# Products of split float32: one 512-column matmul into both halves of a bank in place of two of 256

## Chip, cores and metric

The kernel runs on one core of a Trainium2 chip. The metric is the device time of one execution in microseconds. The core's engines are TensorE (PE, with its weight loads shown as PEld), VectorE (DVE), ScalarE (ACT), GpSimd (POOL) and SyncE (SP, which here only issues DMAs). They run side by side and are ordered by semaphores.

## The reference

A stack of two blocks on 256 tokens of width 1024, all in float32. The first block does twice (depth 2): a half-weighted SwiGLU layer, a mixer (a gated recurrence in depth 0, a spatial gating in depth 1), and a second SwiGLU layer. The second block puts 16 meta tokens ahead (272 rows) and does two layers of windowed attention beside an mLSTM. Most of the arithmetic is in dense products with weights:

```python
def swiglu(x, w_in, w_out):                 # w_in 1024 x 5632, w_out 2816 x 1024
    g, u = jnp.split(x @ w_in, 2, axis=-1)
    return (jax.nn.silu(g) * u) @ w_out

h = h + 0.5 * swiglu(rms_norm(h, ffn1_norm[i]), ffn1_w_in[i], ffn1_w_out[i])
h = h + mixer(rms_norm(h, mix_norm[i]))
h = h + 0.5 * swiglu(rms_norm(h, ffn2_norm[i]), ffn2_w_in[i], ffn2_w_out[i])
```

## The kernel before

**Layout.** Everything is transposed: features on the 128 partitions, tokens on the free axis. The residual `h` holds 8 chunks of 128 features. The norm's gain is applied to the activations and its reciprocal root (`rstd`, one value a token) after the product.

**Split products.** A float32 value is held as two fp32r parts, hi and lo. A product takes three matmuls a block of 128 rows (k): w_hi with x_hi, w_hi with x_lo, w_lo with x_hi, all added in one PSUM tile of 256 (or 272) columns (L526 to L528). Each brings its own weight load. Activations lie in `x_hi`, `x_lo` (input of a layer) and `y_hi`, `y_lo` (input of an output product).

**Units and pairs.** `plan()` cuts all weights into 456 units of up to 4 k blocks x 256 columns, and a pair of output tiles (T = 2 pair + m, m = 0, 1) takes the units of its 256 columns one after another: two units in a gate/up pair, six (4, 4, 4, 4, 3, 3 blocks) in an FFN output pair. Tile T lies in bank T mod 4, so a bank comes back after two pairs; PE then waits for `tile_read`. `first_done` tells that tile m = 0 of a pair is complete, `unit_done` that a unit is.

**Weights.** SP loads a unit into a ring of 4 (`raw`) once the lo part of the unit that had the slot is made. ACT makes w_hi by a cast (L925), three units ahead of PE and not before PE is done with the slot; DVE makes w_lo = raw - w_hi (L1439); PE waits for `lo_made`.

**Gate/up turns.** A phase `in..` is 11 turns of a gate pair and an up pair (the first turn written out, the others a hardware loop on each engine). In a turn DVE multiplies the two gate tiles with rstd (L1479), ACT takes the silu (L961), POOL multiplies it with rstd (L1325), DVE multiplies the up tiles with that (L1495), ACT rounds the result to y_hi (L971) and DVE makes y_lo (L1502). Between them each of ACT and DVE handles four units of weights in a written-out order.

**Output phases.** `out..`, `rec_out`, `sg_out` and `proj..`: for each tile DVE adds the scaled tile to `h` (L1524, an STT), ACT makes x_hi of the next layer (L932) and DVE x_lo (L1452). After the last chunk the sum of squares goes through PE (L552, L554), a root on ACT (L950) and a reciprocal on DVE (L1457).

**Phases in order:** in01, out01, rec_b, rec_a, rec_out, in02, out02, in11, out11, sg_b, sg_a, sg_out, in12, out12, then for each of two layers kv, mif, aq, mqk, mv, mo, ag, mg (with attention and mLSTM steps between the units) and proj0 or proj1. Products from kv to proj0 have 272 columns in part; those of proj1 have 256.

## Time and profile before

| | |
|---|---|
| times of three runs | 1570.74, 1567.24, 1570.32 us |
| median | 1570.32 us |
| profiled execution, first to last instruction | 1566.5 us |
| around that span, by the median | 3.8 us |
| PE / DVE / ACT / POOL busy | 97 / 67 / 49 / 18% of the span |
| read from HBM | 237.21 MB, 152 GB/s over the span |

The profile lists one profiled execution by its span; its own total, with what lies around the span, is not listed apart, and the table gives the difference to the median instead. Matmuls are pipelined: the duration of one (280 ns) overlaps the next ones, so PE's pace is read from the times at which matmuls start, or from how many fall into a stretch. The granted clock of TensorE has two levels here, 1.00 (2.4 GHz) and 0.50 (1.2 GHz). An idle time is put down to what ended it.

### The profile page before, as it was taken

To read this page: it belongs to the slowest core of one execution; us is meant where nothing else is said; L and a number is where in the kernel's file an instruction comes from. 1 tells how busy PE (TensorE), PEld (TensorE's weight loads), DVE (VectorE), ACT (ScalarE), POOL (GpSimd) and SP (SyncE) were. 2 spreads that over 40 slices of the span, in tenths; PEclk is the share of its full clock that TensorE was granted. 3 is DMA by queue.
4 is the path that set the end of the run, shared out by engine and by line. 5 is a ranking of instruction groups with operands and counts; after the bars stand their busy time and mean duration, and the time that the engine had idled before them with its cause. 6 is when DMAs were issued, how large, how long until landed. Compare 5 with 4: busy or idle time off the path is not lost.

```text
span 1566.5 us, 31432 instructions
## 1 busy us (share of the span) xinstructions
PE 1522.4 (97%) x11949; PEld 1463.1 (93%) x11949; DVE 1051.3 (67%) x1997; ACT 768.2 (49%) x1274; POOL 289.2 (18%) x350
## 2 busy tenths in 40 slices
PE   7999998999999999999999998999999999999998
PEld 6999998999999999999999997888898999888898
DVE  6666579766656665567766556896678678765783
ACT  5544457554535454454545434446544453564442
POOL 4111112211111111131311023432100124321000
PEclk9999999999999999999999998999999999999999
DMA  6556753465555655554665553433333543333333
GB/s 202 188 180 197 242 164 122 150 199 179 177 188 173 190 180 182 181 177 134 189 187 182 175 180 94 139 106 95 96 95 108 176 143 115 95 95 109 98 120 120
DMA packets 245275, 239.65 MB, mean 153 GB/s; under 512 B 15160, under 2 KB 244392, under 8 KB 245048
## 3 DMA queue, kind: packets, MB, share of 16 engines
q1 hardware_dynamic: 245176, 238.29, 48.5%
q8 instruction: 67, 1.10, 0.3%
q14 instruction: 32, 0.26, 0.1%
HBM read 237.21 MB, written 1.05 MB: 152 GB/s over the span
## 4 chain that ended last, share of the span: by engine, by line
PE 85%; DVE 10%; ACT 2%; issue 2%; POOL 1%; DMA 0%; SPq 0%; DVEq 0%; ACTq 0%; POOLq 0%
PE bank L526 25%; PE bank L528 25%; PE bank L527 25%; DVE w_lo L1439 2%; PE bank L842 1%; PE bank L801 1%; PE bank L780 1%; PE bank L779 1%; ACT w_hi L925 1%; PE bank L760 1%; DVE work L1592 1%; DVE work L1479 1%; PE bank L847 1%; PE bank L856 0%; PE bank L812 0%
## 5 line engine op out<-in xcount | busy, mean ns | idle before, releaser
L1439 DVE TENSOR_TENSOR w_lo<-raw,w_hi 128x1024 fp32r<-128x1024 f32 (+1 forms) x456 | 556.6, 1229 | 319.0 <-ACT w_hi L925 318.8
L526 PE MATMUL bank<-x_hi,w_hi 128*128 128x256 f32 (+1 forms) x2480 | 722.7, 291 | 6.7 <-DVE x_lo L1452 5.2
L528 PE MATMUL bank<-x_hi,w_lo 128*128 128x256 f32 (+1 forms) x2480 | 709.5, 286 | 0.0
L527 PE MATMUL bank<-x_lo,w_hi 128*128 128x256 f32 (+1 forms) x2480 | 708.7, 286 | 0.0
L925 ACT CAST w_hi<-raw 128x1024 fp32r<-128x1024 f32 (+1 forms) x456 | 465.3, 1029 | 275.9 <-PE bank L528 261.2
L526 PEld LDWEIGHTS bank<-x_hi,w_hi 128*128 128x128 f32 x2480 | 478.2, 193 | 15.8 <-issue 10.9
L527 PEld LDWEIGHTS bank<-x_lo,w_hi 128*128 128x128 f32 x2480 | 478.7, 193 | 0.8
L528 PEld LDWEIGHTS bank<-x_hi,w_lo 128*128 128x128 f32 x2480 | 478.1, 193 | 0.0
L526 PE MATMUL bank<-y_hi,w_hi 128*128 128x256 f32 (+1 forms) x1088 | 311.0, 286 | 8.1 <-DVE y_lo L1450 8.1
L528 PE MATMUL bank<-y_hi,w_lo 128*128 128x256 f32 (+1 forms) x1088 | 310.1, 285 | 0.0
L527 PE MATMUL bank<-y_lo,w_hi 128*128 128x256 f32 (+1 forms) x1088 | 310.0, 285 | 0.0
L526 PEld LDWEIGHTS bank<-y_hi,w_hi 128*128 128x128 f32 x1088 | 209.7, 193 | 9.1 <-DVE w_lo L1439 4.4
L528 PEld LDWEIGHTS bank<-y_hi,w_lo 128*128 128x128 f32 x1088 | 209.8, 193 | 0.0
L527 PEld LDWEIGHTS bank<-y_lo,w_hi 128*128 128x128 f32 x1088 | 209.8, 193 | 0.0
L1325 POOL TENSOR_TENSOR work<-work,rstd 128x256 f32<-128x256 f32 x88 | 63.5, 741 | 417.5 <-ACT work L961 417.5
L1479 DVE TENSOR_TENSOR work<-bank,rstd 128x256 f32<-128x256 f32 (+1 forms) x204 | 82.3, 423 | 21.7 <-PE bank L528 21.2
L971 ACT CAST y_hi<-work 128x256 f32 (+1 forms) x88 | 35.5, 407 | 89.0 <-DVE work L1495 89.0
L961 ACT ACTIVATE work<-work 128x256 f32<-128x256 f32 x88 | 36.0, 418 | 78.5 <-DVE work L1479 78.5
L1306 POOL TENSOR_TENSOR sq<-h 128x256 f32<-128x256 f32 (+1 forms) x48 | 33.4, 696 | 200.2 <-DVE h L1524 197.7
L932 ACT ACTIVATE x_hi<-h,par 128x256 fp32r<-128x256 f32 (+1 forms) x64 | 32.7, 512 | 69.9 <-DVE h L1524 62.3
L1452 DVE SCALAR_TENSOR_TENSOR x_lo<-h,par,x_hi 128x256 fp32r<-128x256 f32 (+1 forms) x64 | 36.3, 569 | 29.5 <-ACT x_hi L932 29.4
L1304 POOL TENSOR_TENSOR sumsq<-h 128x256 f32<-128x256 f32 (+1 forms) x8 | 4.9, 616 | 253.9 <-DVE h L1524 245.9
(259 smaller groups left out, 1244.5 us busy)
## 6 DMA issues: line engine op xcount, KB each, us to landing
raw<-in_ffn_w_in_dram SPq DMA_DIRECT2D x176, 512.0 KB, 3.6
raw<-in_w_in_dram SPq DMA_DIRECT2D x100, 512.0 KB, 3.4
raw<-in_ffn_w_out_dram SPq DMA_DIRECT2D x64, 512.0 KB, 3.8
raw<-in_w_out_dram SPq DMA_DIRECT2D x32, 512.0 KB, 3.5
raw<-in_ffn_w_out_dram SPq DMA_DIRECT2D x32, 384.0 KB, 3.0
raw<-in_rec_w_in_dram SPq DMA_DIRECT2D x16, 512.0 KB, 3.3
raw<-in_sg_w_in_dram SPq DMA_DIRECT2D x16, 512.0 KB, 3.3
raw<-in_rec_w_out_dram SPq DMA_DIRECT2D x8, 512.0 KB, 3.4
```

The lines of the kernel that those rows point to most:

```text
L526: mm(acc, wh, xh, start=first and j == 0, stop=False)
L527: mm(acc, wh, xl, start=False, stop=False)
L528: i_ = mm(acc, wl, xh, start=False, stop=last and j == n - 1)
L925: nc.scalar.copy(w_hi[:, s, 0:n, :], raw[:, s, 0:n, :]).then_inc(hi_made, 1)
L932: i_ = activation(xview(dst, k, N), src, ACT.Copy, scale=scale)
L961: activation(ffn_s[:, m, :], ffn_t[:, m, :], ACT.Silu).then_inc(silu_done, 1)
L971: nc.scalar.copy(dst, ffn_h[:, m, :]).then_inc(act_hi, 1)
L1306: link(TT(sq[:, T0:L], src(c), src(c), MUL))
L1325: TT(ffn_r[:, m, :], ffn_s[:, m, :], rstd[:, META:L], MUL).then_inc(gate_scaled, 1)
L1439: TT(w_lo[:, s, 0:n, :], raw[:, s, 0:n, :], w_hi[:, s, 0:n, :].bitcast(fp32), SUB).then_inc(lo_made, 1)
L1452: i_ = STT(out=xview(dst_lo, k, N), in0=src, scalar=scale, in1=hi, op0=MUL, op1=SUB)
L1479: TT(dst, tile(pr, m, N), rstd[:, T0:L], MUL).then_inc(tile_read, 1)
```

## The change

Eleven phases are marked (`HALVES`): the four gate/up phases, the four FFN output phases, rec_out, sg_out and proj1. In a marked pair a k block takes two matmuls: w_hi with hi and lo of the activations side by side, 512 columns over a whole bank, and w_lo with hi, 256 columns, into the upper half of the bank. The result of a tile is the sum of both halves of its bank. For this x_hi and x_lo become two rows of one tensor `x_s`, and y_hi and y_lo of `y_s`.

In a gate/up turn ACT copies the upper half ("low" terms) to SBUF and DVE adds it to the lower half, for gate and up tiles. Both products with rstd and with the gate then run on POOL: POOL has six products a turn where it had two. In an output phase DVE adds the two halves to `h` in two linked STTs.

```diff
+HALVES = set()
+for _n in ("in01", "out01", "rec_out", "in02", "out02", "in11", "out11", "sg_out", "in12", "out12", f"proj{DEPTH - 1}"):
+    _, _b, _k = PHASES[_n]
+    HALVES.update(range(_b, _b + _k))
...
-        x_hi = sb("x_hi", [P, NC8 * L], fp32r)
-        x_lo = sb("x_lo", [P, NC8 * L], fp32r)
-        y_hi = sb("y_hi", [P, NF * SEQ], fp32r)
-        y_lo = sb("y_lo", [P, NF * SEQ], fp32r)
+        x_s = sb("x_s", [P, 2, NC8 * L], fp32r)
+        y_s = sb("y_s", [P, 2, NF * SEQ], fp32r)
+        x_hi, x_lo = x_s[:, 0, :], x_s[:, 1, :]
+        y_hi, y_lo = y_s[:, 0, :], y_s[:, 1, :]
...
-                        if N == SEQ and wide_x:
-                            xh, xl = (t[:, k * L + META:(k + 1) * L] for t in (hi, lo))
+                        cols = slice(k * L + META, (k + 1) * L) if N == SEQ and wide_x else slice(k * N, (k + 1) * N)
+                        opens, closes = first and j == 0, last and j == n - 1
+                        if pair in HALVES:
+                            both = bank[T % 4][:, :].rearrange("p (h n) -> p h n", h=2)
+                            small = bank[T % 4][:, SEQ:2 * SEQ]
+                            if opens:
+                                mm(both, wh, xs[:, :, cols], start=True, stop=False)
+                                mm(small, wl, xs[:, 0, cols], start=False, stop=False)
+                            else:
+                                mm(small, wl, xs[:, 0, cols], start=False, stop=False)
+                                i_ = mm(both, wh, xs[:, :, cols], start=False, stop=closes)
                         else:
-                            xh, xl = xview(hi, k, N), xview(lo, k, N)
-                        mm(acc, wh, xh, start=first and j == 0, stop=False)
-                        mm(acc, wh, xl, start=False, stop=False)
-                        i_ = mm(acc, wl, xh, start=False, stop=last and j == n - 1)
+                            acc = bank[T % 4][:, 0:N]
+                            mm(acc, wh, xs[:, 0, cols], start=opens, stop=False)
+                            mm(acc, wh, xs[:, 1, cols], start=False, stop=False)
+                            i_ = mm(acc, wl, xs[:, 0, cols], start=False, stop=closes)
...
-            def gate_turn(pb, ub, i, first=None):
-
-                o4, o = 4 * i, (4 * i if not isinstance(i, int) else 4 * i)
+            def low_half(pr, m, i, f, dst):
+
+                U = units_of(pr)[-1][0] + 1
+                if m == 0:
+                    act.wait_ge(first_done, FIRSTS[pr] + 1 + 2 * i)
+                else:
+                    act.wait_ge(unit_done, U + 4 * i)
+                nc.scalar.copy(dst, bank[(2 * pr + m) % 4][:, SEQ:2 * SEQ]).then_inc(low_out, 1)
+
+            def gate_turn(ub, i, f, first=None):
+                pb, count = PHASES[IN_OF[f]][1], SPLITS["y_out" + IN_OF[f][2:]]
+
+                o = 4 * i
                 for U in (ub, ub + 1):
                     split_w(U + LEAD, o)
                 if first is not None:
                     root(first, META)
                 for m in range(2):
-                    act.wait_ge(tile_read, 2 * pb + m + 1 + o4)
+                    low_half(pb, m, i, f, ffn_s[:, m, :])
+                for m in range(2):
+                    act.wait_ge(gate_normed, 22 * f + m + 1 + 2 * i)
                     activation(ffn_s[:, m, :], ffn_t[:, m, :], ACT.Silu).then_inc(silu_done, 1)
                 for U in (ub + 2, ub + 3):
                     split_w(U + LEAD, o)
                 for m in range(2):
-                    act.wait_ge(tile_read, 2 * pb + 2 + m + 1 + o4)
+                    act.wait_ge(act_ready, count + m - 1 + 2 * i)
+                    low_half(pb + 1, m, i, f, ffn_h[:, m, :])
+                for m in range(2):
+                    act.wait_ge(gated_up, 22 * f + m + 1 + 2 * i)
...
                 def turn(i):
+                    for m in range(2):
+                        pool.wait_ge(tile_read, 2 * pb + m + 1 + 4 * i)
+                        TT(ffn_t[:, m, :], ffn_t[:, m, :], rstd[:, META:L], MUL).then_inc(gate_normed, 1)
                     for m in range(2):
                         pool.wait_ge(silu_done, 22 * f + m + 1 + 2 * i)
                         TT(ffn_r[:, m, :], ffn_s[:, m, :], rstd[:, META:L], MUL).then_inc(gate_scaled, 1)
+                    for m in range(2):
+                        pool.wait_ge(tile_read, 2 * pb + 2 + m + 1 + 4 * i)
+                        pool.wait_ge(gate_scaled, 22 * f + m + 1 + 2 * i)
+                        pool.wait_ge(act_ready, count + m - 1 + 2 * i)
+                        TT(ffn_h[:, m, :], ffn_t[:, m, :], ffn_r[:, m, :], MUL).then_inc(gated_up, 1)
...
-                    scaled(pb, m, ffn_t[:, m, :], SEQ, META, o)
+                    dve.wait_ge(low_out, 44 * f + m + 1 + 4 * i)
+                    if f or not isinstance(i, int):
+                        dve.wait_ge(gated_up, 22 * f + m - 1 + 2 * i)
+                    TT(ffn_t[:, m, :], tile(pb, m, SEQ), ffn_s[:, m, :], ADD).then_inc(tile_read, 1)
                 for U in (ub + 2, ub + 3):
                     split_w(U + LEAD, o)
                 for m in range(2):
-                    wait_tile(pb + 1, m, o)
-                    dve.wait_ge(gate_scaled, 22 * f + m + 1 + 2 * i)
-                    TT(ffn_h[:, m, :], tile(pb + 1, m, SEQ), ffn_r[:, m, :], MUL).then_inc(tile_read, 1)
+                    dve.wait_ge(low_out, 44 * f + m + 3 + 4 * i)
+                    dve.wait_ge(silu_done, 22 * f + m + 1 + 2 * i)
+                    TT(ffn_t[:, m, :], tile(pb + 1, m, SEQ), ffn_h[:, m, :], ADD).then_inc(tile_read, 1)
...
-                        STT(out=h[:, c, T0:L], in0=tile(pb + p, m, N), scalar=half, in1=h[:, c, T0:L], op0=MUL,
-                            op1=ADD).then_inc(tile_read, 1)
+                        i_ = STT(out=h[:, c, T0:L], in0=tile(pb + p, m, N), scalar=half, in1=h[:, c, T0:L], op0=MUL, op1=ADD)
+                        if pb + p in HALVES:
+                            link(i_)
+                            i_ = STT(out=h[:, c, T0:L], in0=low(pb + p, m), scalar=half, in1=h[:, c, T0:L], op0=MUL, op1=ADD)
+                        i_.then_inc(tile_read, 1)
```

**PE, the first tile of the program's first marked pair.** Before, three matmuls of 256 columns a k block (two blocks shown):

```order
L526 MATMUL bank<-x_hi,w_hi 128x256
L527 MATMUL bank<-x_lo,w_hi 128x256
L528 MATMUL bank<-x_hi,w_lo 128x256
L526 MATMUL bank<-x_hi,w_hi 128x256
L527 MATMUL bank<-x_lo,w_hi 128x256
L528 MATMUL bank<-x_hi,w_lo 128x256
```

and now, in the same place (the first three blocks):

```order
L532 MATMUL bank<-x_s,w_hi 128x512
L533 MATMUL bank<-x_s,w_lo 128x256
L535 MATMUL bank<-x_s,w_lo 128x256
L536 MATMUL bank<-x_s,w_hi 128x512
L535 MATMUL bank<-x_s,w_lo 128x256
L536 MATMUL bank<-x_s,w_hi 128x512
```

The first block opens the bank with the 512-column matmul; from the second on the 256-column one (w_lo) comes first and the 512-column one (w_hi) closes. One matmul and one weight load a block are gone.

**ACT, the first gate/up turn.** `work` holds all small tiles of the FFN. Before, from the root of the norm on:

```order
L950 ACTIVATE rms<-bank,epsc 128x256
L961 ACT_TABLE_LOAD
L961 ACTIVATE work<-work 128x256 x2
L925 CAST w_hi<-raw 128x1024 x2
L971 CAST y_hi<-work 128x256 x2
```

and now:

```order
L972 ACTIVATE rms<-bank,epsc 128x256
L981 COPY work<-bank 128x256 x2
L995 ACT_TABLE_LOAD
L995 ACTIVATE work<-work 128x256 x2
L947 CAST w_hi<-raw 128x1024 x2
L981 COPY work<-bank 128x256 x2
L1008 CAST y_s<-work 128x256 x2
```

Two copies out of a bank stand ahead of the silu of the gate tiles, and two ahead of the cast to y_hi. The two casts of weights (w_hi) still come between, behind the silu.

**POOL, the loop over turns.** Before:

```order
L1326 ISA
L1325 TENSOR_TENSOR work<-work,rstd 128x256
L1324 REGISTER_ALU
L1325 TENSOR_TENSOR work<-work,rstd 128x256
L1326 REGISTER_ALU
L1326 COMPARE_AND_BRANCH
```

and now, up to the first of the last two products:

```order
L1373 ISA
L1364 TENSOR_TENSOR work<-work,rstd 128x256
L1363 REGISTER_ALU
L1364 TENSOR_TENSOR work<-work,rstd 128x256
L1366 ISA
L1367 TENSOR_TENSOR work<-work,rstd 128x256
L1366 REGISTER_ALU
L1367 TENSOR_TENSOR work<-work,rstd 128x256
L1369 REGISTER_ALU
L1371 REGISTER_ALU
L1372 TENSOR_TENSOR work<-work 128x256
L1369 REGISTER_ALU
```

The product of the gate tiles with rstd (L1364) has moved here from DVE and now stands ahead of ACT's silu; the product of silu with rstd (L1367) was here before; the product with the up tiles (L1372) has moved here too and stands ahead of ACT's cast to y_hi.

## Rows read from the trace of the kernel before

**Rows 1.** The page, part 1: busy us, share of span, instructions of each engine.

```profile
PE 1522.4 (97%) x11949; PEld 1463.1 (93%) x11949; DVE 1051.3 (67%) x1997; ACT 768.2 (49%) x1274; POOL 289.2 (18%) x350
```

**Rows 2.** The page, part 4: the chain that ended last, share by engine.

```profile
PE 85%; DVE 10%; ACT 2%; issue 2%; POOL 1%; DMA 0%; SPq 0%; DVEq 0%; ACTq 0%; POOLq 0%
```

**Rows 3.** The page, part 5, PE: group, count, busy us, mean ns, idle before.

```profile
L526 PE MATMUL bank<-x_hi,w_hi 128*128 128x256 f32 (+1 forms) x2480 | 722.7, 291 | 6.7 <-DVE x_lo L1452 5.2
...
L526 PEld LDWEIGHTS bank<-x_hi,w_hi 128*128 128x128 f32 x2480 | 478.2, 193 | 15.8 <-issue 10.9
...
L526 PE MATMUL bank<-y_hi,w_hi 128*128 128x256 f32 (+1 forms) x1088 | 311.0, 286 | 8.1 <-DVE y_lo L1450 8.1
```

**Rows 4.** Windows, a gate/up stretch: busy us and instructions touching the window.

```profile
core 0: us, PE busy (x) PEld busy (x) DVE busy (x) ACT busy (x) POOL busy (x), PEclk, DMA share, GB/s
320.00:420.00 100.00, 100.00 (x836) 100.00 (x835) 63.01 (x88) 49.84 (x69) 11.56 (x16) 1.00 0.58 181
```

**Rows 5.** Waits of PE: us in total, times, longest us.

```profile
PE bank L526 <- DVE y_lo L1450: 8.1, 5, 4.2
PE bank L526 <- DVE x_lo L1452: 5.2, 3, 4.1
...
PE bank L552 <- POOL sumsq L1307: 2.2, 1, 2.2
```

**Rows 6.** Timeline of PE at half clock: start us, duration us, group.

```profile
270.47 0.41 PE L526 MATMUL bank<-y_hi,w_hi 128*128 128x256 f32 x1
270.69 0.41 PE L527 MATMUL bank<-y_lo,w_hi 128*128 128x256 f32 x1
...
274.10 0.41 PE L528 MATMUL bank<-y_hi,w_lo 128*128 128x256 f32 x1
```

**Rows 7.** Timeline of PE, 272 columns: fp32r products, then plain fp32.

```profile
1063.91 0.29 PE L526 MATMUL bank<-x_hi,w_hi 128*128 128x272 f32 x1
...
1065.67 0.29 PE L528 MATMUL bank<-x_hi,w_lo 128*128 128x272 f32 x1
...
1138.95 0.39 PE L842 MATMUL bank<-work 128*128 128x272 f32 x1
...
1139.18 0.52 PE L842 MATMUL bank<-work 128*128 128x272 f32 x2
```

**Rows 8.** Groups of ACT by form: copies out of a bank.

```profile
L1185 ACT COPY work<-bank 128x256 f32<-128x256 f32 x16 | 5.6, 350 | 0.0
```

**Rows 9.** Timeline of DVE and POOL, a steady gate/up turn.

```profile
105.34 0.42 DVE L1479 TENSOR_TENSOR work<-bank,rstd 128x256 f32<-128x256 f32 x1 [0.24 <-PE bank L528]
107.19 1.23 DVE L1439 TENSOR_TENSOR w_lo<-raw,w_hi 128x1024 fp32r<-128x1024 f32 x1 [1.43 <-ACT w_hi L925]
...
105.62 1.44 POOL L1325 TENSOR_TENSOR work<-work,rstd 128x256 f32<-128x256 f32 x2 [10.07 <-ACT work L961]
```

**Rows 10.** Timeline of DVE, first turn of in02: pairs of w_lo.

```profile
302.31 2.36 DVE L1439 TENSOR_TENSOR w_lo<-raw,w_hi 128x1024 fp32r<-128x1024 f32 x2 [0.76 <-ACT w_hi L925]
...
310.30 2.44 DVE L1439 TENSOR_TENSOR w_lo<-raw,w_hi 128x1024 fp32r<-128x1024 f32 x2 [1.42 <-ACT w_hi L925]
```

**Rows 11.** Timeline where output phases end: out01, out12, proj1.

```profile
209.13 0.42 DVE L1524 SCALAR_TENSOR_TENSOR h<-bank,h 128x256 f32<-128x256 f32 x1
...
211.53 0.48 DVE L1452 SCALAR_TENSOR_TENSOR x_lo<-h,par,x_hi 128x256 fp32r<-128x256 f32 x1 [0.58 <-ACT x_hi L932]
...
212.78 0.28 PE L526 MATMUL bank<-x_hi,w_hi 128*128 128x256 f32 x1
...
951.73 0.75 DVE L1524 SCALAR_TENSOR_TENSOR h<-bank,h 128x256 f32<-128x256 f32 x2
...
1560.60 0.42 DVE L1524 SCALAR_TENSOR_TENSOR h<-bank,h 128x256 f32<-128x256 f32 x1 [1.00 <-PE bank L528]
```

**Rows 12.** Line L1439: count, duration ns min/median/max.

```profile
L1439 DVE TENSOR_TENSOR w_lo<-raw,w_hi x456: 944/1225/1808, 13.4 to 1550.0; 128x1024 fp32r<-128x1024 f32 x140, 128x768 fp32r<-128x768 f32 x12
```

39 lines of the change are left out of this document (21 added, 18 removed).

## Prediction

> **What bounds the kernel now.** I read the busy shares first. PE is busy 97% of the span, DVE 67%, ACT 49%, POOL 18% [rows 1]; the chain that ended last is 85% PE [rows 2]. Next came the groups of PE's instructions: the three products of a k block are 2480 + 1088 triples, 10,704 matmuls [rows 3]. How fast they follow each other is the whole kernel, and neither the busy share nor the mean of 291 ns shows it, since neighbours overlap. The pace is in the counts of a stretch. From 320 to 420 us the clock is 1.00 and 836 matmuls touch a window of 100 us; some 2.4 of them began before it (one lasts 0.28), so one starts each 100/833.6 = 0.1200 us [rows 4]. Check: 10,704 x 0.120 = 1284 us of the span of 1566.5. Last I looked for what PE waits for: 8.1 us for y_lo, 5.2 for x_lo, 2.2 for the sum of squares [rows 5]. Weights are not among the large ones. In a steady turn of a gate/up loop (96 matmuls, 11.52 us) all others have time to spare. So the change is worth what it does to PE's pace, less what it adds at the few places where PE waits.
>
> **What 120 ns consist of.** At the half clock (0.50, which is 1.2 GHz) the same 256-column matmul starts each 0.213 us: from 270.47 to 274.10 are 17 steps, 0.2135 each [rows 6]. That is 256 / 1.2 GHz = 213.3 ns and nothing else. At 2.4 GHz the columns alone would take 106.7 ns, but the pace is 120.0: 13.3 ns are lost on each matmul that brings new weights. With 272 columns the step is (1065.67 - 1063.91)/14 = 0.1257 us [rows 7]: 113.3 of columns and 12.4 lost. A loss proportional to the columns would give 127.5. It is nearly a fixed loss per weight load.
>
> **Part 1, PE: the same columns in two matmuls.** In the marked pairs hi and lo of the activations lie side by side, so w_hi is loaded once for 512 columns and w_lo once for 256. Triples in marked pairs: four gate/up phases of 22 pairs x 8 k x 2 tiles = 1408; four FFN output phases of 4 x 22 x 2 = 704; rec_out and sg_out 2 x 64 = 128; proj1 4 x 16 x 2 = 128. Together 2368 of 3568. The 768 columns of each are as before; one matmul with its load goes. What the 512-column matmul takes no row shows, so it is bounded:
> - Most favourable: the loss is hidden completely under the longer stream. The nearest row: a plain fp32 record of 272 columns, with a 128x128 load under it, starts 0.23 us after its predecessor [rows 7], about 2 x 272 column times (226.7) and only some 3 more. Then 512 columns take 213.3 + 3 = 216, a triple 216 + 120 = 336 instead of 360, and 2368 x 24 = 57 us go.
> - Middle: each load costs its 13 ns, however long the matmul above it. Then 213.3 + 13.3 = 226.7, a triple 346.7, and 2368 x 13.3 = 31.5 us go.
> - Least favourable: loss in proportion to columns (120/256 = 0.469 ns each): 240 ns, a triple 360, nothing goes.
> I take the middle. The 272-column rows decide against both ends: a load that only had to fit under the columns would show less loss with more columns (120 flat, or 113.3 + 3 = 116), and 125.7 was measured, still 12.4 above the columns. That the half clock loses nothing fits too: the stream then reads half as fast and leaves room for the load.
> The Trainium skill speaks for the favourable end: "TensorE: Matmul & The Clock Gate", section "Step-by-step: what each phase is for", says the moving operand and the weight load read SBUF through ports of their own, so a load takes nothing from the running matmul; its section "Back-to-back issue gap" gives N/2.4 + 2.5 ns. By that rule 512 columns take 216 ns and the sum would be -57. By the same rule 256 columns would take 109 and 272 columns 116; the trace has 120.0 and 125.7, so it disagrees here, and I leave the rule as a rival.
>
> **Part 2, the gate/up turn: longer chain, off PE's path.** ACT gains four copies of 128x256 from a bank; the same form takes 350 ns [rows 8], 1.4 us a turn. DVE keeps six operations of the same form. POOL gains four products: two take 1.44 us [rows 9], so six are 4.4 us of a turn. Loads by turn: ACT 49.84/100 x 11.5 = 5.7, now 7.1; DVE 7.3, unchanged [rows 4]. All below 11.1. The latency is what must be checked, because the silu now stands behind a POOL product and ahead of a w_hi on ACT. Today the second gate tile is read at 105.34, right after PE, and the w_lo that follows starts at 107.19 and ends 1.23 later [rows 9], 3.1 us after the tile. Afterwards: copy 0.35, add 0.42, product 0.74, silu 0.42, w_hi 1.05, w_lo 1.23, and some 0.1 for each of six hand-offs: 4.8 us. PE needs this unit three units after the tile, 3 x 2.77 = 8.3 us. Slack 3.5 us, cost 0. The bank of a tile is needed again one pair (5.5 us) after its pair ends and is read within 1.5: cost 0. In the first turn of a phase rstd comes late: in in02 the two w_lo run from 310.30 to 312.74 [rows 10]; copies ahead and products behind delay the first to about 312.9, PE takes it at 313.4 by the new pace. Cost 0, at worst 0.5 us in four phases. Weight loads: the DMA share is 0.58 at 181 GB/s [rows 4]; at the new pace it is 188 GB/s, and slots come free at most 1.7 us later against a turn of slack. Cost 0.
>
> **Part 3, the output phases: one more STT per tile.** Each bank tile is now added in two linked steps of 0.42 (the row of the first [rows 11]). Inside a phase this is hidden: a pair lasts 15.8 us. Where it ends, four places stand in line:
> - out12 to kv0: the two STT that end the phase run in 0.75 us [rows 11], and everything until the new x_lo waits for them; four of them with two links take 1.65. +0.9 us.
> - proj1 to the end: the last STT at 1560.60 [rows 11], now two: +0.45.
> - out01, out02 and out11 to their successors: x_lo of the last chunk ends at 211.53 + 0.48 = 212.0 and PE takes it at 212.78 [rows 11]. It moves by 0.9, so PE waits 0.15 to 0.5 there: about +1 in all. rec_out and sg_out have 1.4 us of slack (two full units in a pair), cost 0.
> With first turns and possible short stretches at the half clock I take +3 us, bounds 1.5 and 8 (a stretch at the half clock costs half its length).
>
> **The sum.** -31.5 + 3 = -28.5 us against the profiled execution: span 1566.5 to 1538.0. What lies around the span is 1570.32 - 1566.5 = 3.8 us by the median of the three runs, which range over 3.5 us; the profiled execution has no total of its own in the rows. The time is 1570.3 - 28.5 = 1541.8.
>
> **The rivals.**
> - **Loads hidden under long matmuls** (-57 + 3): 1516.3. For: the half clock's 213.3 and the fp32 row's 230, both without a loss, both with matmuls over 200 ns. Against: 125.7 at 272 columns. Between the two lies a partial hiding, 1520 to 1535.
> - **The 512-column matmul pays by column** (0 + 3): 1573, no change or hardly slower. For: 120/256 and 125.7/272 differ by only 1.5%; the moving operand now also comes from two places 8.7 KB or 22.5 KB apart. Against: the same two numbers, and the half clock.
> - **The gate/up chain becomes the bound** (slower). Place: ACT's queue in the 44 turns, where silu waits for POOL, and behind it the w_hi of the fifth next unit, its w_lo, and PE. It decides once the 4.8 us exceed 8.3, for instance if POOL's products and DVE's two-operand w_lo block each other and a w_lo of 1.2 takes 2 or 3 (its longest is 1.81 today [rows 12]). Each us beyond costs 44 us: at one us the time is 1570.3 - 28.5 + 44 = 1586. Against: slack is 3.5 us and the two w_lo at 310.30, partly beside POOL, took 2.44 us where two without it, at 302.31, took 2.36 [rows 10].
> The Trainium skill, "SBUF — State Buffer", section "Who interferes with whom", says that a DVE instruction with two SBUF inputs and a reading GpSimd instruction lock each other out entirely. By it each overlap would cost up to 0.74 us; the rows just named show 0.08 for two, so the trace does not bear it out at that size, and even two full blocks would leave 2 us of slack.
>
> **How the numbers follow.** Middle case 0.52; loads hidden, wholly or in part, 0.33; by column 0.09; chain bound 0.03; output hand-overs or clock at their upper bound or other surprises beyond 1560, 0.03. The likeliest gives 1541.8, its own range is 1536 to 1548. The range over cases goes down to the hidden case with some room, 1512, and up to 1562, leaving out the last cases, about 0.14. Within 0.2% (3.1 us, about what a measurement of this kernel can tell from no change) lies most of the by-column case: same 0.08; slower 0.06; faster 0.86.
>
> **What would show it.** Matmuls in all: 11,949 less 2368, 9581. In a steady gate/up stretch the 512-column matmul should be followed after 0.227 us (hidden: 0.216; by column: 0.240) and the 256-column one after 0.120; a turn lasts 11.09 us (10.75; 11.52). DVE and ACT go on waiting, PE does not. PE's waits for the sums of squares and for x_lo grow by some 2 us. If PE waits for w_lo in the loops, the chain rival is right; if the 256-column pace itself leaves 120 beside the longer matmuls, the idea of a fixed loss per load is wrong.

## The result, and the profile after

The changed kernel takes 1574.68 us (median of 12 runs, 1569.85 to 1577.03) and the kernel before 1567.22 (12 runs, 1565.13 to 1570.74): ratio 1.0044, interval 1.0034 to 1.0054. It is slower by 0.4%. 1541.8 was predicted; the time lies above the predicted range too. The profiled spans are 1573.3 and 1566.5.

The page, parts 1 and 4, of the kernel after (answer to [rows 1, 2]):

```profile
PE 1516.1 (96%) x9581; PEld 1338.1 (85%) x9581; DVE 1059.2 (67%) x2053; ACT 809.4 (51%) x1450; POOL 412.3 (26%) x526
...
PE 50%; issue 20%; DVE 15%; ACT 7%; POOL 6%; POOLq 1%; ACTq 0%; DMA 0%; DVEq 0%; SPq 0%
```

The 9581 matmuls are as predicted. But the chain that ended last is 50% PE where it was 85%: ACT, DVE and POOL are on it for long stretches, and the rest is issue. The 1% of busy share that PE lost does not show this at all.

The window of a gate/up stretch (answer to [rows 4]; same columns):

```profile
320.00:420.00 100.00, 99.80 (x562) 85.66 (x561) 61.10 (x89) 57.17 (x105) 35.59 (x50) 1.00 0.57 178
```

562 matmuls touch the window, so some 560.4 start in it; with 64 to a turn that is 11.42 us a turn. It was 11.52 and should have been 11.09. The 11.42 is an average of two regimes, as place 1 below shows.

PE's waits in the kernel after (answer to [rows 5]):

```profile
PE bank L535 <- DVE w_lo L1486: 5.7, 3, 4.0
PE bank L532 <- DVE y_s L1497: 5.6, 2, 4.3
PE bank L539 <- DVE x_s L1499: 5.2, 3, 4.1
PE bank L535 <- DVE x_s L1499: 4.6, 4, 1.9
```

L532 is the 512-column matmul that opens a tile, L535 (w_lo, 256 columns) and L536 (w_hi, 512) the two of every later k block, L539 the first of three in unmarked pairs; L1486 makes w_lo, L1499 and L1497 make the low rows of x_s and y_s. Two entries are new: PE waits for w_lo, and in marked pairs for x_s.

To see where the time goes, I cut the traces at the last matmul of each phase (its start). Times in us; e1, e3, e7 and e9 are experiments below, and rec_b, rec_a, sg_b and sg_a, which aren't marked, are left out:

```
phase     before   after      e1      e3      e9      e7
in01      145.34  144.41  142.53  145.50  144.98  141.88
out01      63.36   69.85   63.75   62.01   69.54   66.38
rec_out    33.72   33.79   33.19   32.64   33.70   33.55
in02      127.57  127.90  126.83  130.29  129.22  124.06
out02      63.36   62.20   62.13   62.01   63.36   61.55
in11      127.57  126.73  125.18  128.02  127.86  125.22
sg_out     25.43   24.86   24.87   24.86   25.41   25.41
in12      127.57  132.24  130.99  131.27  132.28  124.70
out12      63.36   62.19   62.13   62.01   63.36   61.55
kv0        19.01   19.60   18.46   19.62   19.46   19.52
```

Three things stand out. The undisturbed output phases gain 1.17 us, where 2.34 was expected (176 triples by 13.3 ns). The gate/up phases should have gained 4.7 us each; in11 gained 0.8. And two phases lose outright: out01 6.5 us, in12 4.7 us.

**Place 1, the steady gate/up turn.** Timelines of DVE, ACT and POOL after, half a turn:

```profile
382.84 2.36 DVE L1486 TENSOR_TENSOR w_lo<-raw,w_hi 128x1024 fp32r<-128x1024 f32 x2 [0.48 <-ACT w_hi L947]
385.12 0.75 DVE L1536 TENSOR_TENSOR work<-bank,work 128x256 f32<-128x256 f32 x2
388.49 2.36 DVE L1486 TENSOR_TENSOR w_lo<-raw,w_hi 128x1024 fp32r<-128x1024 f32 x2 [2.62 <-ACT w_hi L947]
```

```profile
381.76 2.01 ACT L947 CAST w_hi<-raw 128x1024 fp32r<-128x1024 f32 x2
383.67 0.63 ACT L981 COPY work<-bank 128x256 f32<-128x256 f32 x2
386.39 0.42 ACT L995 ACTIVATE work<-work 128x256 f32<-128x256 f32 x1 [2.09 <-POOL work L1364]
387.09 0.42 ACT L995 ACTIVATE work<-work 128x256 f32<-128x256 f32 x1 [0.28 <-POOL work L1364]
387.42 1.99 ACT L947 CAST w_hi<-raw 128x1024 fp32r<-128x1024 f32 x2
```

```profile
385.62 1.44 POOL L1364 TENSOR_TENSOR work<-work,rstd 128x256 f32<-128x256 f32 x2 [4.39 <-DVE work L1536]
```

Read them as one sequence: casts at 381.76, second w_lo ends 385.20, the adds end 385.87 (they stand behind that w_lo), POOL's products with rstd 385.62 to 387.06, the second silu starts at 387.09, and only behind it come the next two casts, at 387.42. From casts to casts is 5.66 us, and the second half of the turn does the same with the y_hi casts. Over whole turns between 325 and 430 us ACT's casts come back each 11.55 us, in every turn alike. No step waits for PE here: it is a ring of three in-order queues, and 11.55 us is its period. PE's side in the same place:

```profile
383.67 0.39 PE L536 MATMUL bank<-x_s,w_hi 128*128 128x512 f32 x1
384.12 0.39 PE L535 MATMUL bank<-x_s,w_lo 128*128 128x256 f32 x1
384.35 0.39 PE L536 MATMUL bank<-x_s,w_hi 128*128 128x512 f32 x1
```

The step from 383.67 to 384.12 is 0.45 us, every other one behind a 512-column matmul 0.23 to 0.24. The first w_lo of the pair ends at 382.84 + 1.23 = 384.07: PE waits for it. The same happens each 11.5 us from 372 to 430 us. Before 372 PE runs at its own pace, 11.25 us a turn, and uses up the lead of w_lo (from the end of a unit's w_lo to PE's first matmul of that unit): 1.1 us for the unit that PE starts at 327.4, 0.8 at 338.7, 0.5 at 350.0, 0.2 at 361.2, and 0.05 from 372.6 on, where PE waits.

**Place 2, the first units of out01.** PE and DVE after:

```profile
159.23 0.58 PE L535 MATMUL bank<-y_s,w_lo 128*128 128x256 f32 x1 [3.96 <-DVE w_lo L1486]
```

```profile
153.51 0.16 DVE L1621 SCALAR_TENSOR_TENSOR work<-par 128x8 f32<-128x8 f32 x1
...
155.59 1.37 DVE L1615 SCALAR_TENSOR_TENSOR work<-work 128x8 f32<-128x8 f32 x7
...
157.96 4.09 DVE L1486 TENSOR_TENSOR w_lo<-raw,w_hi 128x1024 fp32r<-128x1024 f32 x4
```

Early in out01 DVE runs a 4.4 us chain of small operations on decay constants. The w_lo made ahead used to cover it: PE takes the first unit of out01 5.4 us after its w_lo is done in the kernel before, and 0.4 us after it now. Four w_lo stand behind the chain, and PE waits 3.96 us; then its clock falls:

```profile
140.00:160.00 20.00, 14.32 (x75) 11.60 (x75) 12.16 (x33) 10.95 (x18) 4.27 (x6) 0.98 0.51 162
160.00:170.00 10.00, 10.00 (x52) 8.62 (x51) 5.55 (x8) 2.62 (x3) 0.61 (x1) 0.87 0.80 245
```

In the first window PE is busy 14.32 of 20 us, and in the second the granted clock is 0.87. The lead can have gone by the ring's period or by a tile's longer way to the casts; e9 looks at that.

**Place 3, in12 behind sg_out.** DVE in sg_out, one pair of units, and PE where in12 begins:

```profile
758.20 2.36 DVE L1486 TENSOR_TENSOR w_lo<-raw,w_hi 128x1024 fp32r<-128x1024 f32 x2 [0.46 <-ACT w_hi L947]
760.48 0.41 DVE L1571 SCALAR_TENSOR_TENSOR h<-bank,h 128x256 f32<-128x256 f32 x1
760.93 0.42 DVE L1574 SCALAR_TENSOR_TENSOR h<-bank,h 128x256 f32<-128x256 f32 x1
761.94 0.48 DVE L1499 SCALAR_TENSOR_TENSOR x_s<-h,par,x_s 128x256 fp32r<-128x256 f32 x1 [0.58 <-ACT x_s L954]
...
764.74 2.36 DVE L1486 TENSOR_TENSOR w_lo<-raw,w_hi 128x1024 fp32r<-128x1024 f32 x2 [0.46 <-ACT w_hi L947]
```

```profile
769.01 0.38 PE L535 MATMUL bank<-x_s,w_lo 128*128 128x256 f32 x1 [1.93 <-DVE x_s L1499]
...
770.87 0.58 PE L535 MATMUL bank<-x_s,w_lo 128*128 128x256 f32 x1 [1.24 <-DVE x_s L1499]
```

From w_lo pair to w_lo pair DVE takes 764.74 - 758.20 = 6.54 us; PE wants a pair each 5.6. Over the phase DVE falls behind, and in12 pays: two waits for x_s, and 770 to 780 us at a granted clock of 0.66.

### The profile page after: what moved, and what is told of

Same layout as the page of the kernel before. It is cut to its first block, busy times and chain, and to the rows that moved or that the text cites. A ratio compares the mean times of both kernels' runs of the same rounds, so it can differ in the third digit from the quotient of the medians.

```text
span 1573.3 us, 27747 instructions
## 1 busy us (share of the span) xinstructions
PE 1516.1 (96%) x9581; PEld 1338.1 (85%) x9581; DVE 1059.2 (67%) x2053; ACT 809.4 (51%) x1450; POOL 412.3 (26%) x526
## 4 chain that ended last, share of the span: by engine, by line
PE 50%; issue 20%; DVE 15%; ACT 7%; POOL 6%; POOLq 1%; ACTq 0%; DMA 0%; DVEq 0%; SPq 0%
PE bank L536 12%; PE bank L539 7%; PE bank L541 7%; PE bank L540 7%; PE bank L535 6%; ACT w_hi L947 4%; DVE w_lo L1486 4%; POOL work L1364 3%; DVE work L1542 2%; POOL work L1372 2%; PE bank L855 1%; ACT work L981 1%; PE bank L814 1%; PE bank L793 1%; PE bank L792 1%
## 5 line engine op out<-in xcount | busy, mean ns | idle before, releaser
L1486 DVE TENSOR_TENSOR w_lo<-raw,w_hi 128x1024 fp32r<-128x1024 f32 (+1 forms) x456 | 547.0, 1225 | 285.6 <-ACT w_hi L947 285.0
L536 PE MATMUL bank<-x_s,w_hi 128*128 128x512 f32 x1232 | 444.4, 398 | 0.0
L535 PE MATMUL bank<-x_s,w_lo 128*128 128x256 f32 x1232 | 350.2, 284 | 6.4 <-DVE x_s L1499 4.6
L539 PE MATMUL bank<-x_s,w_hi 128*128 128x256 f32 (+1 forms) x1072 | 322.8, 301 | 5.4 <-DVE x_s L1499 5.2
L536 PE MATMUL bank<-y_s,w_hi 128*128 128x512 f32 x904 | 325.2, 401 | 0.0
L541 PE MATMUL bank<-x_s,w_lo 128*128 128x256 f32 (+1 forms) x1072 | 310.2, 289 | 0.0
L540 PE MATMUL bank<-x_s,w_hi 128*128 128x256 f32 (+1 forms) x1072 | 309.4, 289 | 0.0
L536 PEld LDWEIGHTS bank<-x_s,w_hi 128*128 128x128 f32 x1232 | 232.8, 189 | 45.5
L535 PE MATMUL bank<-y_s,w_lo 128*128 128x256 f32 x904 | 256.9, 284 | 8.1 <-DVE w_lo L1486 5.0
L535 PEld LDWEIGHTS bank<-x_s,w_lo 128*128 128x128 f32 x1232 | 234.0, 190 | 24.7 <-DVE w_lo L1486 8.8
L539 PEld LDWEIGHTS bank<-x_s,w_hi 128*128 128x128 f32 x1072 | 207.1, 193 | 14.3 <-issue 9.8
L540 PEld LDWEIGHTS bank<-x_s,w_hi 128*128 128x128 f32 x1072 | 207.5, 194 | 0.8
L541 PEld LDWEIGHTS bank<-x_s,w_lo 128*128 128x128 f32 x1072 | 206.9, 193 | 0.0
L536 PEld LDWEIGHTS bank<-y_s,w_hi 128*128 128x128 f32 x904 | 172.1, 190 | 38.6
L535 PEld LDWEIGHTS bank<-y_s,w_lo 128*128 128x128 f32 x904 | 173.1, 191 | 13.4 <-DVE w_lo L1486 6.4
L1364 POOL TENSOR_TENSOR work<-work,rstd 128x256 f32<-128x256 f32 x88 | 63.2, 740 | 202.6 <-DVE work L1536 202.6
L1372 POOL TENSOR_TENSOR work<-work 128x256 f32<-128x256 f32 x88 | 63.2, 739 | 126.9 <-DVE work L1542 126.9
```

The source lines that it names most:

```text
L535: mm(small, wl, xs[:, 0, cols], start=False, stop=False)
L536: i_ = mm(both, wh, xs[:, :, cols], start=False, stop=closes)
L539: mm(acc, wh, xs[:, 0, cols], start=opens, stop=False)
L540: mm(acc, wh, xs[:, 1, cols], start=False, stop=False)
L541: i_ = mm(acc, wl, xs[:, 0, cols], start=False, stop=closes)
L1364: TT(ffn_t[:, m, :], ffn_t[:, m, :], rstd[:, META:L], MUL).then_inc(gate_normed, 1)
```

## The experiments

Each shared its chip with runs of the kernel before, whose medians were 1566.9 to 1568.1.

**e1, one weight cast ahead of each wait for POOL.** In a gate/up turn ACT makes a w_hi before the silus and one before the y_hi casts, not both behind them (the two added lines stand ahead of the waits for POOL; an FFN output phase leaves out the one cast that is made already).

```diff
-                for U in (ub, ub + 1):
-                    split_w(U + LEAD, o)
+                if isinstance(i, int):
+                    split_w(ub + LEAD, o)
+                split_w(ub + 1 + LEAD, o)
...
+                split_w(ub + 2 + LEAD, o)
...
-                for U in (ub + 2, ub + 3):
-                    split_w(U + LEAD, o)
+                split_w(ub + 3 + LEAD, o)
...
+                split_w(ub + 4 + LEAD, o)
```

> Theory A (closed chain): a gate/up turn of the changed kernel (11.5 us) is set by a ring through the in-order queues of ACT, DVE and POOL: two copies out of a bank, w_lo in DVE's way, the add, two POOL products, silu (or the cast to y_hi), then two weight casts that stand behind it, twice a turn. Moving one weight cast ahead of each wait for POOL (it is ready by then) takes 1.0 us out of each half of the ring, so PE's pace becomes the bound again: 32 x (234 + 118 ns) = 11.26 us a turn. Phases in02 and in11 go from 127.9 and 126.7 to about 124.5 us, the waits of 4.4 us at out01 and 2.3 and 1.6 us at in12 go or shrink; in all 1574.7 - 9 - 8 = about 1558 us. Rival B (pace alone): the loops are bound by the matmuls' own pace, the waits are chance: in02 stays near 127.9, in all within 3 us of 1574. Rival C (transfers): w_lo is late since weights land later (4.3 us median instead of 3.6): the order on ACT does not matter, no change.

Measured: 1561.76 us (5 runs), ratio 0.9967 (0.9954 to 0.998), faster than before and 13 us faster than the change. The steady stalls are gone, out01 is 63.75, and the window of 320 to 420 us holds 569 matmuls, 11.28 us a turn:

```profile
320.00:420.00 100.00, 100.00 (x569) 86.83 (x568) 66.14 (x91) 62.11 (x110) 48.28 (x56) 1.00 0.62 192
```

The same work in another order on one queue gives this, so the ring and not any engine's load was the bound, nor the landing of the weights. in11 comes to 125.18 us, near the 124.5 expected, but in02 stays at 126.83 and in12 at 130.99: that is place 3, which this edit leaves (e7), and the time is 4 us above the 1558 expected. Something else shows here. In the changed kernel POOL's products and w_lo take turns, in e1 they overlap, and both last longer:

```profile
385.67 1.47 DVE L1489 TENSOR_TENSOR w_lo<-raw,w_hi 128x1024 fp32r<-128x1024 f32 x1 [0.43 <-ACT w_hi L947]
386.03 2.41 POOL L1370 TENSOR_TENSOR work<-work,rstd 128x256 f32<-128x256 f32 x2
```

A w_lo alone takes 1.23 us and two such products 1.45. Over the trace 46 of POOL's products take 1.71 us on average instead of 0.74, each with about 1.1 us of w_lo beside it.

**e2, the chain made longer.** ACT copies each low half of the gate tiles twice.

```diff
+                if twice:
+                    nc.scalar.copy(pre[:, m, 3:3 + SEQ], bank[(2 * pr + m) % 4][:, SEQ:2 * SEQ])
```

> The changed kernel with two more copies of 128x256 out of a bank on ACT in each gate/up turn, ahead of those that the add waits for (their result is not used). Theory A: each costs 0.3 to 0.35 us in the ring: +0.65 us a turn, 44 turns, +28 us: 1602; in02 from 127.9 to about 135. Rival B (pace alone) and C (transfers): ACT has 4 us of slack a turn, so no change beyond 2 us.

Measured: 1575.87 (4 runs), ratio 1.0058 (1.0043 to 1.0072), as without the copies. The expectation was missed, but the timeline above says why: ACT's copies (383.67) lie beside the w_lo pair on DVE (until 385.20), behind which the adds stand anyway. The dose was put beside the ring: in its own trace, too, ACT's casts come back each 11.54 us. It also shows that ACT has room.

**e3, only the output phases widened.**

```diff
-for _n in ("in01", "out01", "rec_out", "in02", "out02", "in11", "out11", "sg_out", "in12", "out12", f"proj{DEPTH - 1}"):
+for _n in ("out01", "rec_out", "out02", "out11", "sg_out", "out12", f"proj{DEPTH - 1}"):
```

> 512-column products only in the output phases (960 of the 2368 triples); gate/up turns as before the change. Theory A and B alike: 960 x 8.3 ns = 8.0 us less on PE, 2.4 us more where output phases end, none of the ring's waits: 5.6 us less than before the change, about 1561.6; in phases at 127.6 as before, the four FFN output phases 62.2 each (out01 too, where the changed kernel has 69.9). If it is not faster than before, what the second STT adds at the ends of phases was put too low.

Measured: 1569.62 (12 runs), ratio 1.0012 (1.0003 to 1.0021). The expected 1561.6 was missed, and the phases point to place 3: each FFN output phase gained 1.35 us, out01 too, but in02 and in12, which did not change, took 2.7 and 3.7 us more. Which of the widened phases hands this on, e7 tells.

**e4, the pace alone.** A kernel of its own that leaves out the reference's computation: rows of matmuls on resident operands, each with a new weight tile (one run, like e8 and e10).

> A kernel of its own that leaves the reference's computation out and only runs streams of matmuls with new weights each, one after another at the full clock, each form on a line of its own. Times from start to start. Theory F (one fixed loss of 13.3 ns per weight load): 256 columns 120.0, 272 columns 126.7, 384 columns 173.3, 512 columns 226.7, in one piece or in two. Theory S (two places): 512 in one piece 226.7, in two pieces 8.7 KB apart 234. Theory G (loss grows with the columns): 512 in one piece 234 to 240, 384 about 176 to 180. Theory H (the load is what the matmul waits for): 512 columns 216. With 64 columns of weights in place of 128 the loss at 256 columns halves to 6.7 under F and G, and is 2.5 under H. Plain float32 256 columns: 216 a record. With DVE and ACT busy on 128x1024 operations nothing changes (as in the kernel), unless the loss comes from them; then 120 without them was never reached.

Timeline of PE (start, duration, line, count):

```profile
24.79 5.92 PE L58 MATMUL bank<-xs,w 128*128 128x256 f32 x48
30.55 11.07 PE L60 MATMUL bank<-xs,w 128*128 128x512 f32 x48
41.46 11.04 PE L62 MATMUL bank<-xs,w 128*128 128x512 f32 x48
52.34 0.39 PE L65 MATMUL bank<-xs,w 128*128 128x512 f32 x1
...
60.69 8.49 PE L71 MATMUL bank<-xs,w 128*128 128x384 f32 x48
69.02 6.16 PE L73 MATMUL bank<-xs,w 128*128 128x272 f32 x48
75.01 5.63 PE L75 MATMUL bank<-xs,w 128*64 128x256 f32 x48
80.48 10.52 PE L77 MATMUL bank<-raw_x,raw_w 128*128 128x256 f32 x48
```

Each row's pace is the distance to the next row's start over its count: 256 columns (30.55 - 24.79)/48 = 120.0 ns; 512 columns in two pieces (52.34 - 41.46)/48 = 226.7; 384 columns 173.5; 272 columns 124.8. So in a row of one width a load costs 13.3 ns at 256, 384 (settled) and 512 columns: the prediction's middle case to the tenth. It is not the same at every width: at 272 columns it is 11.5, and a last row of 128 columns takes 111.6 ns a matmul, 58 above its columns. But from 52.34 to 60.69 stand 24 matmuls of 512 and 23 of 256 columns in turn, which should take 8.20 us and take 8.35: a pair of neighbours takes 352.8 ns, not 346.7. The Trainium skill, "TensorE: Matmul & The Clock Gate", section "Back-to-back issue gap", gives N/2.4 + 2.5 ns for a matmul by itself, 109 and 216 here, and for a stream of loads and matmuls about 81 ns at 128 columns and 131 at 512. The prediction took the first for the rule of a stream. The rows of this case agree with neither: 111.6 at 128 columns, 120.0 at 256, 226.7 at 512.

**e5, a dose on the ring.** One extra product of POOL ahead of the gate products, once a turn.

```diff
+                        if m == 0:
+                            TT(pre[:, 0, 3:3 + SEQ], ffn_t[:, m, :], rstd[:, META:L], MUL)
```

> The changed kernel, with one more product of POOL (256 columns, some 0.74 us, written to a buffer that nothing reads there) ahead of the gate product in every gate/up turn. The previous experiment put its extra copies beside the loop; this one is put on it. Theory A (the in-order queues of ScalarE, VectorE and POOL form a closed loop in a gate/up turn: weight casts, second w_lo, add, two POOL products, casts again, 11.55 us a turn against the 11.27 us of TensorE's own matmuls): the turn goes to 11.55 + 0.74 = 12.3 us wherever the three units of lead are used up, so PE waits about 1.0 us a turn and each of the four gate/up phases grows by 7 to 8 us; about 1604 us in all. Theory B (nothing but TensorE's pace sets the turn, and the waits in the changed kernel are an accident of the phases' borders): no change, 1575 us. Theory C (POOL's queue is free enough but its SBUF accesses slow VectorE): below 1585.

Measured: 1602.9 us (4 runs), ratio 1.0225 (1.021 to 1.0241), against 1604 expected by the ring and 1575 by its rival. PE's wait for w_lo goes from 3 times to 40:

```profile
PE bank L535 <- DVE w_lo L1488: 22.9, 40, 4.0
```

ACT's casts now come back each 12.23 us. POOL is busy 28% of that span; 0.74 us more of it a turn costs 28 us. With e1 the ring is shown from both sides.

**e6, matmuls of one width together.** e1, and in a unit's tile four 512-column and four 256-column matmuls in two groups.

```diff
+                        wide_first = first or m == 1
+                        for turn_ in range(2):
+                            for j in range(n):
...
+                                if wide_first == (turn_ == 0):
+                                    i_ = mm(both, wh, xs[:, :, cols_of(j)], ...)
+                                else:
+                                    i_ = mm(small, wl, xs[:, 0, cols_of(j)], ...)
```

> The kernel of the first experiment (one weight cast ahead of each wait for POOL) with one more edit: in a unit's tile the four 512-column matmuls stand together and the four 256-column ones together, the order of the two groups alternating from tile to tile, so that the width changes once a tile and not eight times. Theory A (alternating widths cost about 6 us per 1000 pairs over what the two matmuls take in a row of their own: 352.8 against 346.7 ns): a pair falls from about 352 to about 348 ns, the 2368 pairs give back 9 to 12 us, about 1551 us. Theory B (the loss comes with each weight load whatever the widths are, and the pairs of the model were only slowed by the two pieces of the 512-column operand): no change, 1562 us. Theory C (grouping makes the first four matmuls of a unit need both weight halves of all four k blocks later or sooner, and new waits take the gain): pairs shorter in the profile but the time within 2 us of 1562.

Measured: 1560.31 (5 runs), ratio 0.9949 (0.9935 to 0.9963); e1's interval overlaps it, so no gain is shown. out02 goes from 62.13 to 61.55, 3.3 ns a triple, about half of what e4 left to be had (352.8 - 346.7), and out01, rec_out and sg_out lose 1.5, 1.3 and 0.7.

**e7, e6 with rec_out and sg_out as before the change.**

```diff
-for _n in ("in01", "out01", "rec_out", "in02", "out02", "in11", "out11", "sg_out", "in12", "out12", f"proj{DEPTH - 1}"):
+for _n in ("in01", "out01", "in02", "out02", "in11", "out11", "in12", "out12", f"proj{DEPTH - 1}"):
```

> The previous kernel with the two mixer output phases (rec_out and sg_out) taken out of the set that uses 512-column products, so that they run as before the change: each of their pairs of units has two scalar_tensor_tensor, x_hi, x_lo and six weight operations on VectorE and ScalarE, more than the 5.6 us that TensorE wants a pair with the wider products. Theory A (those phases hand a lag to the gate/up phase behind them): in02 falls by about 2.7 us and in12 by about 3.7 us and part of the half-clock time after it, rec_out and sg_out give up 0.5 us each; about 5 to 6 us less than the grouped kernel, 1546 us. Theory B (the waits at the start of in02 and in12 come from the first units of those phases themselves): no gain, or 1 us more, about 1552 us.

Measured: 1552.67 (4 runs), ratio 0.9902 (0.9887 to 0.9917), 7.6 us below e6; in02 fell by 2.35 and in12 by 4.6 us. The 1546 expected counted on a faster e6, and the total alone would fit the rival's 1552; the phases decide. Place 3 is shown: the price of the wider mixer outputs was paid in the phase behind them.

**e8, why mixed widths cost more.** Again a kernel without the reference's computation, with rows of mixed widths.

> A kernel of its own that leaves out the whole computation of the reference (its output is meaningless): rows of fp32r matmuls with resident operands, so that only TensorE's pace shows. Known from the last one: 256 columns 120.0 ns start to start, 512 columns 226.7 ns, alternating 512/256 352.8 ns a pair. Theory A (a change of width costs, about 3 ns at each change): groups 512,512,256,256 take 346.7 + 3 = 350 ns a pair and groups of four 348.3 ns; 384/256 alternating 293.3 + 6 = 299; 512/384 alternating 400 + 6 = 406; 320/256 also about 6 above its parts. Theory B (a 256-column matmul behind a 512-column one cannot have its weights loaded early enough, a cost of the pair): only steps behind a 512-column matmul lose, about 9.4 ns each, so groups of two lose 4.7 a pair and 384/256 little or nothing. Theory C (the two-piece operand is what costs beside a narrow one): the contiguous 512/256 row shows 346.7.

None of the three theories holds. From the starts in the trace, a pair takes 293.3 ns with 384/256 (no loss), 266.6 with 320/256 (none), 413 with 512/384 (13 above 400), 348.5 with 512,512,256,256 and 351 in groups of four. So it isn't the change of width. In e4, a row by itself shows a 512-column matmul start its successor after 234, 236, 228, 232, 231 and then always 226.7 ns: it settles after about five, and among others it never gets there. One row came out unexpected (L88, 256 columns at offset 16, operands 320 columns apart; L90 starts behind it):

```profile
72.92 3.79 PE L88 MATMUL bank<-xs,w 128*128 128x256 f32 x32
76.54 4.86 PE L90 MATMUL bank<-xs,w 128*128 128x320 f32 x32
```

(76.54 - 72.92)/32 = 113.1 ns, not 120.

**e9, the new way out without the wide matmuls.** The changed kernel with each 512-column matmul as two of 256 (shown for the block that opens a bank; the later ones likewise).

```diff
-                                mm(both, wh, xs[:, :, cols], start=True, stop=False)
+                                mm(lower, wh, xs[:, 0, cols], start=True, stop=False)
+                                mm(small, wh, xs[:, 1, cols], start=False, stop=False)
```

> The changed kernel with each 512-column matmul written again as two of 256 columns (w_hi by x_hi into the lower half of the bank, w_hi by x_lo into the upper half); the copies of the low half, the VectorE adds of it and the order of both queues stay as the change left them. It separates the gain of the wide matmul from the cost of the new way out of the banks. Theory A (a triple costs 360 ns again instead of 352 to 347; the ring of casts, w_lo, add and POOL products of 11.5 us a turn now lies under TensorE's 11.5 us a turn): about 1568 + 2 to 5 us for what the chains cost at the borders of the phases, 1570 to 1576 us, so that the net gain of the wide matmuls in the changed kernel is about nothing. Theory B (the chains cost their full 13 us wherever they stand, as the difference of 20 us between the matmuls' saving and the time says): 1588 to 1595 us.

Measured: 1580.34 (6 runs), ratio 1.0082 (1.0062 to 1.0101), between both expectations. The copies, adds, second STTs and moved products alone cost 12 us, of which out01 and in12 have most. In a gate/up stretch PE keeps its full pace, because the ring is hardly slower than PE's 11.52 us a turn, at most 0.03 us:

```profile
320.00:420.00 100.00, 100.00 (x835) 100.00 (x835) 61.18 (x90) 57.03 (x105) 35.63 (x50) 1.00 0.58 179
```

The lead of w_lo (for the second unit of each pair) stays at 1.4 to 1.7 us all through in02, and in in01 it falls from 1.7 to 1.1. But it is short from the first turns on, where the kernel before has 5.2: the casts now stand behind the longer way of a tile. For DVE's chain in out01 that is too little:

```profile
158.43 0.58 PE L537 MATMUL bank<-y_s,w_lo 128*128 128x256 f32 x1 [3.79 <-DVE w_lo L1489]
```

So the wait in out01 doesn't need the ring to be slower than PE: a late cast suffices. (The lead of out01's first unit is 5.4 us before, 4.2 in e1, 1.0 here and 0.4 in the changed kernel; the wait behind DVE's chain is none, 1.36, 3.79 and 3.96.) And the wide matmuls, on top of this, bring only 1580.3 - 1574.7 = 5.7 us.

**e10, where the operands lie.**

> A kernel of its own that leaves out the whole computation of the reference (its output is meaningless): rows of fp32r matmuls with resident operands. In the last one a row of 256-column matmuls whose operands began 16 columns off a multiple of 64 and 320 apart took 113.3 ns each, not 120.0, and the loss of alternating rows was 0 for 384/256 and 320/256, 6 for 512/256 and 13 for 512/384, so it isn't the change of width. Rows here: 256 columns at offsets 0, 4, 16, 64, 128 and apart 256 or 320; weights at offset 16; 512 columns at offset 16; 512 columns with every second weight tile; 512/256 alternating at offset 0, at offset 16 and with one weight tile for both; the kernel's triple as three 256-column matmuls at offsets 0 and 16. Theory A (the place of the moving operand in SBUF against that of the weights decides how much of a weight load shows): offset 16 gives 113.3 for every 256-column row and 220 for the 512-column row, the alternating pair 339 or less, and weights at offset 16 change the 120.0 too. Theory B (a distance of 320 columns between successive operands decides): offset 0 with 320 apart gives 113.3 and offset 16 with 256 apart gives 120.0. Theory C (every second weight tile decides): the 512-column row with every second tile shows 233 ns and the pair with one tile for both 346.7.

A kernel of rows again. Worked out from the starts, second half of each row, offsets in columns of 4 bytes: 256 columns at offset 0, 64 or 128 take 120.0 ns, also 320 apart; at offset 16 117.8, at offset 4 118.7; with the weights at offset 16 and the operand at 0, 113.3. 512 columns take 233.3 at offset 16 and 226.7 with every second weight tile; the alternating pair about 353 with two weight tiles or one, and about 349 at offset 16. The kernel's old triple, three matmuls of 256 columns, takes 360 at offset 0 and 353.4 at offset 16: as little as the new pair. Theories B and C fall. Of A holds that the place counts, not its numbers: for 512 columns offset 16 is worse. And e8's odd row, offset 16 and 320 apart, takes 117.8 here and not 113.1; the operands lie 512 bytes further from the weights' start in this kernel, and whether that is why isn't shown.

**e11, the kernel before with w_hi and w_lo 16 columns further in SBUF.** No instruction changes.

```diff
+        gap_a = sb("gap_a", [P, 16])
         w_hi = sb("w_hi", [P, RING, KU, CU], fp32r)
         w_lo = sb("w_lo", [P, RING, KU, CU], fp32r)
+        gap_b = sb("gap_b", [P, 48])
```

(The two small tensors `sinks` and `neg_sinks` move in front of gap_b, so that all behind, the activations too, shifts by 512 bytes.)

> The kernel before the change, with the two weight rings w_hi and w_lo placed 16 columns (64 bytes) further in SBUF against x_hi, x_lo, y_hi and y_lo; no instruction changes. In the rows of the last experiment 256-column matmuls whose weights lay so took 113.4 ns start to start and not 120.0. Theory A (where weights and moving operand lie against each other sets how much of a weight load shows, in the kernel too): 10394 full-clock matmuls by up to 6.6 ns is up to 69 us, and by the 117.8 that other offsets gave 23 us: 1500 to 1545 us, less what other queues then can't keep up with. Theory B (with the kernel's order of operands, two weight tiles and two moving tiles in turn, or with the other engines at work, the effect is gone): 1566 to 1568 us.

Measured: 1546.95 (4 runs), ratio 0.9861 (0.9832 to 0.989):

```profile
330.00:430.00 100.00, 100.00 (x852) 1.00 0.61 184
```

The same window of the kernel before has x836, as [rows 4]: the step falls from 120.0 to about 117.7 ns, which over some 8450 such steps at the full clock is 20 us, the whole gain. Steps of 272 columns stay at 126 ns.

**e12, e7 with that shift.**

> The fastest kernel so far (casts ahead of the waits for POOL, narrow and wide matmuls grouped, mixer output phases as before the change; 1552.7 us) with the same shift of the weight rings by 16 columns. Theory A (the place of the operands counts): the 256-column steps outside the wide phases and the wide triples both shrink, at most 6.6 ns each on 5925 and 2235 steps, 54 us, but the in phases are then bound by the closed loop of the other queues at 11.3 us a turn; 1515 to 1545 us. Theory B (no effect in the kernel): 1552 us. A third way (the 512-column rows got slower at offset 16, 233.4 against 226.7, and the shift may hit them so): up to 1565 us.

Measured: 1547.19 (4 runs), ratio 0.9873 (0.9849 to 0.9897). The shift gives e7 5.5 us where it gave the kernel before 21. The narrow steps gain, while the 512-column ones go from 231.2 to 232.5 ns (means in the trace). With the operands placed so, no gain of the widening is left to be seen: e11, which has none of it, is as fast, and the two intervals overlap. The traces say where it goes: out02 takes 61.01 us here and 62.19 in e11, in02 122.93 and 125.37, but out01 66.95 and 62.19, since DVE's chain still makes PE wait there (4.07 us).

## Why the prediction was wrong

Measured +7.5 us, predicted -28.5: 36 us apart. (The times themselves, 1574.7 and 1541.8, are 32.9 apart: the prediction started from three runs with a median of 1570.3, 3.1 above that of all twelve.) From both traces: the triples gave back some 20 us; the steps between matmuls with weights that exceed the pace of their clock by more than 60 ns, which are PE's waits and its other work, grew by 21.6 us; and the stretches at the half clock grew by 9.7 us (42.5 to 52.3), of which about half is cost. That is -20 + 21.6 + 4.9 = +6.5, beside +6.8 between the spans.

- **Part 1, the size of the middle case: mis-sized.** A fixed 13.3 ns for each load is right in rows of 256 and of 512 columns (e4), if not at 272 (11.5) or 128 (58). The step that failed was to add the two paces: 226.7 + 120.0 = 346.7. In turn they take 352.8 alone, and in the kernel 234.2 + 117.1 = 351.3. So 2368 triples give 20 us, not 31.5. (The 256-column step had left 120, the sign that the prediction named against a fixed loss.) The rivals on PE are both out: hidden loads would be 336, by column 360.
- **Part 2, "Slack 3.5 us, cost 0": failed, and this is the main step.** The working followed one tile to one w_lo, 4.8 us against a lead of 8.3, and compared the engines' loads with the turn. Neither asks the question that counts: does the next round of the chain begin only when this one has ended? It does, since the casts stand behind the silus on ACT, the adds behind w_lo on DVE and the silus behind POOL. Such a ring has a period, 11.55 us, whatever the lead is; the lead only says how many turns pass before it shows. Against PE's old 11.52 it is all but hidden (e9), against the new 11.25 it isn't. e1 and e5 show it from both sides. The slack was also put too high: in in01 the tightest w_lo has 1.4 us in the second turn and 0.05 in the sixth, not 3.5. And it was not free: DVE's chain in out01 lived on it (e9).
- **The third rival named the right place and the wrong point of decision.** It had silu waiting for POOL, behind it w_hi, w_lo and PE, but was to decide at a latency over 8.3 us, and so got 0.03. The prediction's own sign for it, PE waiting for w_lo in the loops, came. Its price of 44 us for each us beyond was about right in kind: e5 paid 28 us for 0.74. Its trigger, POOL and w_lo blocking each other, was put aside with the two w_lo at 310.30, "partly beside POOL"; but POOL's two products (309.07, 1.45 us) end at 310.52 there, so they share 0.22 us and decide nothing. e1 shows that they do slow each other down. It was not what bound the changed kernel, whose ring keeps them apart.
- **First turns and borders, "+3, bounds 1.5 and 8": failed.** The new way out alone costs 12 us (e9). "Inside a phase this is hidden: a pair lasts 15.8 us" holds for the FFN's. "rec_out and sg_out have 1.4 us of slack (two full units in a pair), cost 0" is wrong: DVE's 6.54 us for 5.6 of PE comes up as waits in in02 and in12 (e3, e7). The start of out01, where DVE's chain of constants needs w_lo made ahead, was not looked at; it costs 6.5 us.
- **What held:** 9581 matmuls; kv0 +0.6 us (0.9 predicted); the end, where two STTs now close the kernel from 1566.98, 6.4 us before the end of the span against 5.9 before: +0.4 (0.45 predicted).

Some things stay open: what in the chip sets the 234 to 227 ns that a row of 512-column matmuls goes through, why an offset that helps 256 columns hurts 512, and why the same shift gives 113.3 ns in a row by itself and 117.7 in the kernel. And of the 12 us of e9 only out01's share has its wait shown; in12's is taken from e3 and e7. How the 6.5 us of out01 divide between the ring's period and the late cast isn't separated further than by e9.

## What to carry to other kernels

Before an operation is moved to an idle engine, follow the in-order queues until they close: if casts wait for a product, the product for an add and the add for the last casts, add the whole ring up and compare it with the turn of the bounding engine after the change, not before. When such a ring binds, move the weight work ahead of the wait rather than trimming it. Before a lead is spent, ask which later stretch lives on it. A lag made in one phase is paid in the next, so the phases must be timed one by one, and a pace read from rows of one shape must be measured again for the mix.
